# A hybrid encoder layer on one core: mixer projections as quads in one group behind the first norm, with convolution, gates and q/k passed through DRAM

## The reference

```python
x = layer_norm(ALPHA * x + 0.5 * swiglu(x, ffn1_w_up, ffn1_w_down), ln1_g, ln1_b)
cb, cc, ch, q, k, v, g, gc, gr = jnp.split(x @ w_in, offsets, axis=-1)
yc, new_buf = short_conv(cc * ch, conv_buf, conv_w)          # causal, 3 taps
y_conv = (cb * yc) @ w_conv_br
o, S_new = retention_seq(rotary(q), rotary(k) * DK ** -0.5, v, S0)   # 4 heads, DK 256, DV 512
y_ret = (group_norm(o) * jax.nn.silu(g)) @ w_ret_br
m = jax.nn.sigmoid(gc) * y_conv + jax.nn.sigmoid(gr) * y_ret
x = layer_norm(ALPHA * x + m @ w_out, ln2_g, ln2_b)
x = layer_norm(ALPHA * x + 0.5 * swiglu(x, ffn2_w_up, ffn2_w_down), ln3_g, ln3_b)
```

## Time and profile before

| | us |
|---|---|
| median of 3 runs (1907.19 to 1911.12) | 1907.99 |
| the profiled execution | 1910.33 |
| its span, first to last instruction | 1908.5 |
| PE busy, 11200 instructions | 1845.0 |
| DVE busy | 1109.1 |
| POOL busy | 649.6 |
| ACT busy | 463.0 |
| mean granted TensorE clock | 0.988 |

### The profile page before, as it was taken

The page is one execution under the profiler, slowest core; times in us unless marked ns, Lnnn a source line. Parts: engine busy times, 40 slices in busy tenths (PEclk is TensorE's granted clock), DMA queues, the critical chain, the costliest instruction groups (busy, mean ns, idle before and its releaser), DMA issues. The chain is left out here.

```text
span 1908.5 us, 26753 instructions
## 1 busy us (share of the span) xinstructions
PE 1845.0 (97%) x11200; PEld 1718.0 (90%) x11200; DVE 1109.1 (58%) x1395; ACT 463.0 (24%) x771; POOL 649.6 (34%) x428
## 2 busy tenths in 40 slices
PE   6999999998999999999999999999997999999996
PEld 6989899897889989989989999999986899899895
DVE  6768476577455455355354455334438777585666
ACT  3325234241051051051051000000004234242240
POOL 5324233222423423423423443444432333233230
PEclk9999999998999999999999999999998999999998
DMA  7432423313637637637637544444454423323312
GB/s 289 126 132 75 133 89 114 129 36 132 241 133 254 207 133 254 207 133 254 207 133 257 173 155 144 147 151 155 153 171 152 133 89 122 122 80 131 122 45 99
DMA packets 90328, 286.80 MB, mean 150 GB/s; under 512 B 8928, under 2 KB 11360, under 8 KB 89952
## 3 DMA queue, kind: packets, MB, share of 16 engines
q1 hardware_dynamic: 37376, 133.45, 22.5%
q0 software_dynamic: 24768, 90.19, 13.2%
q10 hardware_dynamic: 28064, 61.45, 8.8%
HBM read 260.86 MB, written 24.19 MB: 149 GB/s over the span
## 5 line engine op out<-in xcount | busy, mean ns | idle before, releaser
L399 POOL TENSOR_TENSOR wl<-raw,wh 128x1024 fp32r<-128x1024 f32 x172 | 436.8, 2540 | 88.7 <-DMA wh<-in_weights 86.0
L461 PE MATMUL ps<-xh,wl 128*128 128x320 f32 x1280 | 401.5, 314 | 30.1 <-POOL wl L399 22.8
L461 PE MATMUL ps<-xh,wh 128*128 128x320 f32 x1280 | 400.1, 313 | 0.0
L461 PE MATMUL ps<-xl,wh 128*128 128x320 f32 x1280 | 400.0, 313 | 0.0
L390 POOL DMA_DIRECT2D wh<-in_weights x172 | 96.8, 563 | 859.7 <-PE ps L461 807.3
L461 PEld LDWEIGHTS ps<-xh,wl 128*128 128x128 f32 x1280 | 244.6, 191 | 33.2 <-POOL wl L399 17.7
L461 PEld LDWEIGHTS ps<-xl,wh 128*128 128x128 f32 x1280 | 244.4, 191 | 0.4
L461 PEld LDWEIGHTS ps<-xh,wh 128*128 128x128 f32 x1280 | 244.2, 191 | 0.0
L461 PE MATMUL ps<-th,wql 128*128 128x320 f32 x640 | 197.7, 309 | 0.0
L461 PE MATMUL ps<-th,wqh 128*128 128x320 f32 x640 | 197.7, 309 | 0.0
L461 PE MATMUL ps<-tl,wqh 128*128 128x320 f32 x640 | 197.4, 309 | 0.0
(11 more groups left out here) (179 smaller groups left out, 3462.3 us busy)
## 6 DMA issues: line engine op xcount, KB each, us to landing
raw<-in_weights SPq DMA_DIRECT2D x172, 512.0 KB, 3.7
wh<-in_weights POOLq DMA_DIRECT2D x172, 512.0 KB, 4.8
qraw<-in_quads SPq DMA_DIRECT2D x80, 512.0 KB, 3.6
state<-in_state_ret ACTq DMA_DIRECT2D x48, 512.0 KB, 7.9
out_ret_sample<-state ACTq DMA_DIRECT2D x32, 512.0 KB, 5.2
z_scratch<-z ACTq DMA_DIRECT2D x1, 2560.0 KB, 8.8
z<-z_scratch ACTq DMA_DIRECT2D x1, 2560.0 KB, 9.7
z<-in_x_prompt ACTq DMA_DIRECT2D x1, 2048.0 KB, 15.9
```

Of the source, the lines that this page charges most:

```text
L399: pool.tensor_tensor(wl[:, r, :], raw[:, r, :], wh[:, r, :].bitcast(f32), ALU.subtract).then_inc(chunk_split, 1)
L461: ins = nc.tensor.matmul(out, lhs, rhs, start=start, stop=stop, skip_group_check=adds)
```

## The change

1. 25 quads (the table PROJECTIONS) replace 50 units: cc, ch, cb, q, k of all heads, and ten tiles of the gates. They are one group, in a new stage behind norm 1, between four gate units (gc 0 and 1, gr 0 and 1) and two more (gr 6 and 7).
2. q and k of the four heads go from the result tiles to DRAM (`spill`) and come back by ACT's queue ahead of each head (`qk_load`), and are rotated from SBUF. A head has no q and k units.
3. Convolution and its product with cb are made by DVE between the quads (`after_projection`). The eight w_conv units follow the stage; DVE multiplies them by sigmoid(gc), which SP loads back from DRAM, into mix, which ACT stores.
4. The gates gr and mix come back in the last head by ACT's queue; DVE merges there, between the branches, and writes m into xh and xl, from which w_out is made. The stages conv and merge go, and the memset of yr.
5. ACT keeps xin at norm 1 too. POOL issues three wh loads ahead at the beginning of the new stage and of FFN 2.

The core of the diff:

```diff
+PROJECTIONS = [(what, j) for j, gates in enumerate((("gc1", "gr1"), ("gc2", "gr2"), ("gc3",), ()))
+               for what in ("cc", "ch", "q", "k") + gates + ("cb",)]
+QUAD_COUNT = (QUADS, len(PROJECTIONS), QUADS)
+QUAD_GROUP = (4, len(PROJECTIONS), 4)
...
 # SP
+            def projections():
+                load_quad(1)
+                load_quad(1)
+                load(6)
+                load_quad(1)
+                load(1)
+                sync.wait_ge(gate_made, 4)
+                sync.dma_start(a["gate_c"][:, 0:2, :], yr[:, 0:2, :]).then_inc(gates_saved, 16)
+                sync.dma_start(a["gate_r"][:, 0:2, :], yr[:, 2:4, :]).then_inc(gates_saved, 16)
+                for q in range(1, len(PROJECTIONS)):
+                    load_quad(1)
+                    spill(q - 1)
+                sync.wait_ge(conv_ready, KT)
+                sync.wait_ge(gates_saved, 32)
+                for p in range(2):
+                    sync.wait_ge(spilled[p], 16 * spills(len(PROJECTIONS), p))
+                for m in range(0, KT, 2):
+                    sync.dma_start(yr[:, m:m + 2, :], a["gate_c"][:, m:m + 2, :]).then_inc(gate_c_in, 16)
+                load(2)
+                sync.wait_ge(gate_made, GATES)
+                sync.dma_start(a["gate_r"][:, 6:8, :], tiles_of(ccbuf)).then_inc(last_gates_saved, 16)
+                load(KT - 3)
...
 # POOL
             def ffn(k):
+                if k == 1:
+                    high(ck(3))
                 low()
...
 # PE
             def head(i):
                 u0 = bk.at
-                starts = i == 0
-                if starts:
-                    first_units()
-                for _ in range(2 * starts, 4):
-                    unit_of_chunk()
                 natural(4, xh, xl)
                 head_wait()
...
+            def projections():
+                first_units()
+                for _ in range(2):
+                    unit_of_chunk()
+                for q in range(len(PROJECTIONS)):
+                    quad(PROJ + q)
+                for _ in range(2):
+                    unit_of_chunk()
+                unit_of_chunk(zh, zl, lambda half, k: pe.wait_ge(conv_ready, k + 1))
+                for _ in range(KT - 1):
+                    unit_of_chunk(zh, zl)
...
-            for _ in range(3 * KT):
-                unit_of_chunk()
-            for _ in range(KT):
-                unit_of_chunk()
-                unit_of_chunk()
-                pe.wait_ge(conv_ready, KT)
-                unit_of_chunk(zh, zl)
             for half in range(2):
-                natural(4, mh, ml, lambda k: pe.wait_ge(conv_ready, KT + k + 1), ends_stage=half == 1)
+                natural(4, xh, xl, lambda k: pe.wait_ge(merged_ready, k + 1), ends_stage=half == 1)
...
 # ACT, head
+                if i == H - 1:
+                    act.wait_ge(last_gates_saved, 16)
+                    act.wait_ge(mix_saved, 16 * 4)
+                    for n, ms in enumerate((slice(0, 2), slice(2, KT))):
+                        act.dma_start(gate_r[:, ms, :], a["gate_r"][:, ms, :]).then_inc(gate_r_in[n], 16)
+                        act.dma_start(mix[:, ms, :], a["mix"][:, ms, :]).then_inc(mix_in[n], 16)
...
                 state_load(i, 0)
+                if i < H - 1:
+                    act.wait_ge(psum_full, u0 + U_S0)
+                    qk_load(i + 1)
+                else:
+                    merge_hi(range(6))
                 state_store(i, 0, range(4), u0 + U_S0)
...
 # DVE
+            def after_projection(q):
+                what, j = PROJECTIONS[q]
+                c = result_tile(q)
+                dve.wait_ge(psum_free, bk())
+                if what == "ch":
+                    step(tt(ccbuf[:, :, :], ccbuf[:, :, :], c[:, :, :], ALU.mult))
+                if what in ("q", "k"):
+                    conv_prompt(j, "qk".index(what))
+                if PROJECTIONS[min(q + 1, len(PROJECTIONS) - 1)][0] == "cb":
+                    conv_sample(j)
+                if what == "cb":
+                    after()
+                    dve.wait_ge(gates_saved, 32)
+                    tt(yr[:, 2 * j:2 * j + 2, :], tiles_of(c), tiles_of(cy),
+                       ALU.mult).then_inc(conv_made, 1)
...
 # DVE, last head
+                branch(2)
+                merge(0)
+                for m in range(1, 5):
+                    branch(m + 2)
+                    merge(m)
+                    merge_lo(m - 1)
+                merge(5)
+                merge_lo(4)
+                branch(KT - 1, SKIPPED)
                 new_state(range(4), 3)
```

More of the change, by code:

```diff
@@ L55, with operand_order @@
 SLOT = {A11: 0, S12: 1, A12: 3, S3: 4, A22: 5, S4: 6}
-def operand_order():
+def operand_order(stage):
     order = [(0, what) for what in range(6)]
-    for q in range(QUADS):
-        starts, ends = q % 4 == 0, q % 4 == 3
-        if starts and q + 1 < QUADS:
+    quads, group = QUAD_COUNT[stage], QUAD_GROUP[stage]
+    for q in range(quads):
+        starts, ends = q % group == 0, q % group == group - 1
+        if starts and q + 1 < quads:
             order.append((q + 1, A11))
-        if q + 1 < QUADS:
+        if q + 1 < quads:
@@ L66, in operand_order @@
             order += [(q + 1, S12), (q + 1, A12), (q + 1, S3)]
-            if not ends and q + 2 < QUADS:
+            if not ends and q + 2 < quads:
                 order.append((q + 2, A11))
             order += [(q + 1, A22), (q + 1, S4)]
+    assert len(order) == len(set(order)) == 6 * quads
     return order
-ORDER = operand_order()
-PLACE = {item: n for n, item in enumerate(ORDER)}
-assert len(PLACE) == len(ORDER) == 6 * QUADS
-def made(ffn, q, what):
-    return 6 * QUADS * ffn + PLACE[q, what] + 1
+PLACE = [{item: n for n, item in enumerate(operand_order(stage))} for stage in range(3)]
@@ L83, with chain_order @@
 P1, P6, P7, P4 = range(4)
-def chain_order():
+def chain_order(stage):
     order = []
-    for q in range(QUADS):
-        if q % 4 == 0:
+    quads, group = QUAD_COUNT[stage], QUAD_GROUP[stage]
+    for q in range(quads):
+        if q % group == 0:
             order.append((q, P1))
         order += [(q, P6), (q, P7)]
-        if q % 4 != 3:
+        if q % group != group - 1:
             order.append((q + 1, P1))
         order.append((q, P4))
+    assert len(order) == len(set(order)) == 4 * quads
@@ L108, in operand @@
 def operand(n, what):
-    return made(n // QUADS, n % QUADS, what)
+    stage = stage_of(n)
+    return 6 * QUAD_START[stage] + PLACE[stage][local(n), what] + 1
 def bank_roles(b):
@@ L188, in quad_tile, with result_tile @@
             return ct[n][:, :, 0:HALF]
+        pm = Region(h_at)
+        ccbuf, cy = pm.take("ccbuf", [128, 4, HALF]), pm.take("cy", [128, 4, HALF])
+        ctp = [pm.take(f"ctp{n}", [128, 4, HALF]) for n in range(2)]
+        def result_tile(q):
+            return ccbuf if PROJECTIONS[q][0] == "cc" else ctp[q % 2]
         hm = Region()
@@ L975, in to_T @@
                         x = four(ps[:, b, :])
-                        if keeps:
-                            copy(xin[:, part[0], part[1]], x).then_inc(x_kept, 1)
+                        copy(xin[:, part[0], part[1]], x).then_inc(x_kept, 1)
                         result(copy(xh[:, part[0], part[1]], x))
@@ new lines, in conv_prompt @@
+            def conv_prompt(j, m):
+                u, y, c = tile(ccbuf, m), tile(cy, m), 2 * j + m
+                after()
+                dve.wait_ge(conv_made, j)
+                step(V.tensor_scalar(y[:, 0:NP], u[:, 0:NP], conv_weight(2, c), None, ALU.mult))
+                for n in (1, 0):
+                    late = 2 - n
+                    after()
+                    step(V.scalar_tensor_tensor(out=y[:, late:NP], in0=u[:, 0:NP - late], scalar=conv_weight(n, c),
+                                                in1=y[:, late:NP], op0=ALU.mult, op1=ALU.add))
@@ L1596, in _ @@
-            for i in range(2):
-                conv(i)
-            def merge(i):
-                for jj in range(4):
-                    s, f = jj % 2, bass.ds(i * 4 + jj, 1)
-                    full(4)
-                    act_result()
-                    dve.wait_ge(conv_ready, i * 4 + (KT + jj))
-                    tt(cz[:, 0, :], cy[:, s, :], one(yr[:, f, :]), ALU.mult).then_inc(psum_free, 4)
-                    dve.wait_ge(psum_free, bk())
-                    b = full(2)
-                    step(tt(two(csb[:, s, :]), pair(b), two(csb[:, s, :]), ALU.mult))
-                    after()
-                    tt(cz[:, 0, :], cz[:, 0, :], csb[:, s, :], ALU.add).then_inc(psum_free, 2)
-                    dve.wait_ge(psum_free, bk())
-                    split(one(mh[:, f, :]), one(ml[:, f, :]), cz[:, 0, :]).then_inc(conv_ready, 1)
@@ L1613, in _ @@
-            for i in range(2):
-                merge(i)
             dve.wait_ge(z_in, 48)
@@ L1759 @@
     args["z_scratch"] = nc.dram_tensor("z_scratch", (128, TT, D), mybir.dt.float32, kind="Internal").ap()
```

(3 more changed lines are left out.)

513 lines of the change are left out of this document (326 added, 187 removed).

## The result

| | before | changed |
|---|---|---|
| median of the runs, us | 1907.59 (1907.14 to 1911.12, 4 runs) | 1922.46 (1918.86 to 1923.94, 4 runs) |
| ratio of the times, 95% interval | | 1.0067 (1.0055 to 1.0080) |
| span of the profiled execution, us | 1908.5 | 1922.1 |
| mean granted clock | 0.988 | 0.975 |

The account below looks back on a forecast made before the run. TensorE (PE), busy 97% of the span, was taken as the bound. Terms -44.0 + 5.1 + 1.7 + 9.5 + 3 + 18 - 3.5 = -10.2 us took the median from 1907.99 to 1898 us, range 1874 to 1912.

Parts of the forecast that it names:

- Matmuls: Projections: 25 quads in place of 50 units take 300 matmuls from PE, 44.0 us less, held certain.
- quads: New stage of 25 quads: DVE keeps PE's pace, 1 us lost plus 0.7 for a copy, +1.7 us (0 to 8).
- norm 1: First norm: longer waits for tiles, lower clock and first quad's operands, less one chunk wait, +5.1 us (3 to 8).
- rival 4: Quads: DVE falls behind at FFN's 13.1 us each, +20 us, 1918 us; chance 0.05.
- the term for the lower clock: First norm: PE's clock falls behind the longer wait before the late half, 1.7 us.
- Rival 1: Queues keep up: last head costs 5, w_conv 1, heads 0; -34.7 us, 1873 us (1868 to 1884); chance 0.22.
- The step to w_conv: Between quads and w_conv: a chunk queued behind gate_c comes late, wait 7.4 us plus 2.1 lower clock, +9.5 (0 to 13).
- Heads 1 to 3: V alone must hide both rotations, head_ready near 25.5 us after V's start; 1 us per head, +3 (0 to 10).
- rival 2: Heads 1 to 3: table ht lands over 16.3 us behind V's start; at 22 us costs 17, 1912 us; chance 0.09.
- rivals 2 and 3: Heads 1 to 3: late table ht, costing 17, chance 0.09; rotations held by POOL at the shared port, +9, chance 0.06.
- The last head: First high copy waits behind stores queued after gate_r and mix; branches freed 15.5 us late, 2.5 lower clock, +18 (5 to 24).
- Norm 2: Second norm: early wh loads remove the 6.10 us wait for the second chunk's split, -3.5 us (-5 to 0).

Follow-up runs that it names:

- e7: Changed kernel, with POOL's splits at both norms held until DVE has scaled the third early tile of z; ratio to the kernel before 1.0056.
- all_five: Changed kernel with edits to last head, w_conv step and both norms, qx made behind k's rotation, z reloaded in halves for w_out; ratio to kernel before 0.9872, 1885.48 us.
- all_seven: all_five plus next head's q and k loaded some 35 us earlier, and two chunks loaded before the first quads at FFN 1's end; 0.9836, 1876.46 us.
- e3: Changed kernel, DVE rotates k before q and waits for ht only after both; does not compute the layer; ratio to the kernel before 1.0046.
- e4: Changed kernel, last head: ACT loads six gate_r/mix tiles behind the state loads, DVE frees branches 5 to 7 before merging tiles 2 to 7; 1.0006, repeated 1.0004.
- six_no_tail: all_seven without the edit that loads two chunks before the first quads at FFN 1's end; ratio to the kernel before 0.9813, 1873.45 us.

## Why the prediction was wrong

**Matmuls, quads, norm 1: right.** 44.0 us are gone; the quads' own waits are 0.5 us (forecast 1.7, rival 4 at 20); norm 1 +5.5 (forecast 5.1), though the make-up differed. The wait before the third tile grew from 5.5 to 8.3 us, which no term had, since two early splits stretched DVE's passes (e7). In its place the term for the lower clock, 1.7, did not come (PE is busy 37.6 us in this stretch before and after), and the wait before the first quad is 1.1, not 2.0. That the sum fits is luck. Rival 1, in which the queues keep up, is out.

**The step to w_conv: +15.2, forecast 9.5.** The mechanism was right: SP's order, the sum of the queues. Three sizes in it were off. gate_c was issued 11.4 us behind the last quad, not 8.4. By the time the chunk had landed the queues had moved 9.4 MB and not 8.1 (367 GB/s over 25.5 us, the first row below; its columns are those of the windows above). So the chunk was split at 844.3 and the wait was 12.2, not 7.4. And the lower clock cost about 3, not 2.1. The rate itself was not too high: 408 GB/s from the issue of gate_c on (the second row), against the 388 of the sum.

```profile
816.40:841.90 25.50, 15.75 (x108) 15.49 (x106) 6.75 (x10) 2.78 (x4) 1.10 (x2) 0.90 0.98 367
822.30:841.90 19.60, 9.85 (x68) 9.59 (x66) 0.88 (x2) 1.34 (x2) 0.53 (x1) 0.87 1.04 408
```

The Trainium skill, DMA: Bandwidth & Descriptors, section Where 436 GB/s comes from, gives 435 GB/s as the ceiling of the sixteen SBUF ports of DMA, and says that between HBM and SBUF some 358 bind. The 412 GB/s over 12 us of this trace lie below the first and above the second, so the 358 did not bind here.

**Heads 1 to 3: +10.6, forecast 3.** The failed step is the count from V's start: "q and k have been loaded by then or 1 us later", and 8.7 us for a rotation. They landed 6.6 us behind V's start in head 1 and 8.4 in head 2. A rotation with one stretched pass took 9.1 to 9.3 us, and with two, as q's in heads 2 and 3, 11.3 and 11.9. ht was there 18.6 us behind V's start in head 1 and not 16, and 21.9 in head 3, where rival 2 begins at 16.3. So rivals 2 and 3 were both partly true and came together, with q and k late on top. Each alone was priced, at +17 and +9 in all; I had given the pair no case. The 10.6 us are 8.1 of waits and 2.5 of longer steps of PE, at most 1.7 of them at the lower clock in head 2 (half of 3.4 us). Of the causes the late q and k are the one that is isolated: all_five and all_seven, both with ht out of the way, differ in the heads by when q and k are loaded, and take 383.1 and 372.3 us. What ht costs by itself is not settled: e3, without its wait, was 4 us faster, and all_five gained nothing in the heads. The Trainium skill, SBUF — State Buffer, section Who interferes with whom, states that a DVE instruction with two SBUF inputs contends with a GpSimd instruction that reads SBUF; the rotation's passes of 2.9 to 3.3 us beside a split agree. The CAST, with one input, was held too (2.98 us); it does 1280 columns in 0.83 us where a two-input pass does 640 in 0.82, and the section leaves one-input instructions out of contention only outside the two-port performance modes.

**The last head: +27, forecast 18.** The largest miss, 9 us; the failed step is the path behind the first high copy. The place, the two orders and the wait were as forecast: first high copy at 1370.5, behind stores that took 19.8 us. What was mis-sized stands behind the copy. The waits for the branches are 12.0 and 6.7 us, 18.8 in sum and not 15.5: 3.3 more. A wait of 3.9 us for a chunk of w_out, loaded beside the reload of z, was not in the sum at all. The rest, 4.3 us, is mostly the lower clock, put at 2.5: some 2 us behind these waits, the others behind the wait of 4.2 us at head 3's transposes and behind the 3.9. In e4 this stretch is 17 to 20 us shorter, and in six_no_tail, which also reloads z in halves, it is 148.0 us: 23 of the 27 are order.

**Norm 2: -1.0, forecast -3.5.** The wait of 6.1 us for the split went and one of 2.1 for the low parts took its place, the -4.0 of the sum. But the wait before the third tile, which I had left as it was, grew from 3.1 to 5.5 us, as the splits now fall on DVE's passes over z (2.7 in e7), and 0.8 came before the second tile. Before, and changed:

```profile
1440.00 1.97 PE L680 MATMUL ps<-ident,z 128*128 128x128 f32 x8 [3.05 <-DVE z L1347]
...
1451.55 1.09 PE L811 MATMUL ps<-ident,z 128*128 128x128 f32 x8 [0.81 <-DVE z L1627]
1458.14 1.12 PE L811 MATMUL ps<-ident,z 128*128 128x128 f32 x4 [5.50 <-DVE z L1627]
```

**The sum.** So the terms of the step to w_conv, heads 1 to 3, the last head and norm 2 were all too low, by 5.7, 7.6, 9 and 2.5 us; with 0.4 at norm 1, less 1.2 for the quads, that is the miss of 24 us between -10.2 and +13.6. The lower clock is not what they have in common. The granted clock was 0.50 for 97.5 us in all, 47.8 before, but that cost 8.9 us of PE's time, and the sum had 6.3 for it (1.7, 2.1 and 2.5). The waits grew by 48.8 us, where the sum had 27.5: 21 of the 24 us lie in waits that came later or in greater number than counted. At w_conv, in the heads and in the last head they are waits behind transfers; in the heads and at norm 2 also behind DVE passes beside a split. I gave 0.22 to a case in which all waits are small, and none to one in which all are larger.

## What to carry to other kernels

When work is taken from the bounding engine, list what it had been covering, transfers first, and ask for each when it is issued, not only how long it takes: here some 49 us came back by six edits of order and place, with no large operation less. A wait in the middle of an in-order list (ACT for stores, DVE for a merge's input, POOL for sums) is paid by all behind it, so the instructions that free PE's banks belong ahead of it. An estimate of several new waits needs a case in which they are all too small.

## What was not expected of the hardware

- A pass of DVE that takes 0.8 us lasts 2.9 to 3.5 beside a split of POOL of 2.4 us, about the two together, whether two-input or a CAST.
- The first transposes come at 449.8 to 454.2 us over the profiles of all kernels without the edit at FFN 1's end, though the program is the same up to there: between two single profiles 4 us can be chance.
- Stores of 0.5 MB that were issued behind 5.2 MB of loads in the same queue took 19.8 us to land; the one issued just ahead of them took 3.2.
